# Two rows of projection unit 15 are queued ahead of the last row of unit 14

## The reference

```python
proj = x @ w_in[l]
q, fz, iv, g, u = jnp.split(proj, [D_HGRN, 2 * D_HGRN, 3 * D_HGRN, 4 * D_HGRN], axis=-1)
o_a, sa = hgrn2_mixer(q, fz, iv, g, ...)    # 4 heads of 128: gated recurrence, RMSNorm, * sigmoid(g)
o_b, sr, si = s5_mixer(u, ...)              # y = gelu(...); y * sigmoid(y @ w_glu)
mix = jnp.concatenate([o_a, o_b], axis=-1) @ w_out[l]
x = layer_norm(ALPHA * x + mix, ln1_g[l], ln1_b[l])
```

## Time and profile before

| | us |
|---|---|
| median of 3 runs | 1201.9 (1201.84 to 1202.13) |
| the profiled execution, its own time | 1201.42 |
| its span in the profile | 1199.7 |
| PE busy in the span | 1170.7 (98%) |
| DVE busy | 815.1 (68%) |
| ACT busy | 508.1 (42%) |

### The profile page before, as it was taken

The page is one execution under the profiler, slowest core; times in us unless marked ns, Lnnn a source line. Parts: engine busy times, 40 slices in busy tenths (PEclk is TensorE's granted clock), DMA queues, the critical chain, the costliest instruction groups (busy, mean ns, idle before and its releaser), DMA issues.

```text
span 1199.7 us, 24092 instructions
## 1 busy us (share of the span) xinstructions
PE 1170.7 (98%) x9718; PEld 1129.7 (94%) x9718; DVE 815.1 (68%) x1498; ACT 508.1 (42%) x850; POOL 180.2 (15%) x152
## 2 busy tenths in 40 slices
PE   9999999999898999999999999999999999999996
PEld 8988889998798999999999999999999999999995
DVE  6995767567888557799627863686458844786547
ACT  5411212337746536675314541354125521554335
POOL 5210000100000244200210021001200030001365
PEclk9999999999899999999999999999999999999999
DMA  8441223518344410411372127222631255122503
GB/s 299 118 122 50 87 79 122 175 61 225 115 109 182 178 36 26 153 37 45 86 261 90 55 64 273 97 66 55 235 137 55 56 181 190 57 57 59 207 25 119
DMA packets 84815, 139.31 MB, mean 116 GB/s; under 512 B 26360, under 2 KB 52504, under 8 KB 84696
## 3 DMA queue, kind: packets, MB, share of 16 engines
q1 hardware_dynamic: 84704, 137.77, 36.0%
HBM read 97.89 MB, written 40.03 MB: 115 GB/s over the span
## 4 chain that ended last, share of the span: by engine, by line
PE 86%; DVE 8%; ACT 2%; issue 2%; DMA 1%; POOL 0%; SPq 0%; POOLq 0%; ACTq 0%; DVEq 0%
PE psum L1984 31%; PE psum L1668 16%; PE psum L1956 15%; PE psum L1687 6%; PE psum L2067 5%; PE psum L1745 4%; PE psum L1657 1%; DVE R L2594 1%; PE psum L1798 1%; PE psum L1780 1%; PE psum L1793 1%; DMA raw<-in_w_units 1%; PE psum L1865 1%; PE psum L1827 1%; DMA raw<-in_w_up 1%
## 5 line engine op out<-in xcount | busy, mean ns | idle before, releaser
L1984 PE MATMUL psum<-XH,wh 128*128 128x258 f32 x640 | 181.4, 283 | 2.5 <-DVE TR L2599 1.5
L1984 PE MATMUL psum<-XH,wl 128*128 128x258 f32 x640 | 181.0, 283 | 0.0
L1984 PE MATMUL psum<-TR,wh 128*128 128x258 f32 x640 | 181.0, 283 | 0.0
L1984 PE MATMUL psum<-XL,wh 128*128 128x258 f32 x640 | 179.8, 282 | 0.0
L1598 POOL TENSOR_TENSOR wl<-raw,wh 128x512 fp32r<-128x512 f32 (+2 forms) x36 | 57.7, 1608 | 567.3 <-ACT wh L1273 556.6
L1984 PEld LDWEIGHTS psum<-XH,wh 128*128 128x128 f32 x640 | 121.0, 189 | 3.2 <-issue 3.2
L1956 PE MATMUL psum<-AH,wl 128*128 128x344 f32 x384 | 123.1, 320 | 0.0
L1956 PE MATMUL psum<-AL,wh 128*128 128x344 f32 x384 | 123.1, 320 | 0.0
L1956 PE MATMUL psum<-AH,wh 128*128 128x344 f32 x384 | 122.9, 320 | 0.0
L1984 PEld LDWEIGHTS psum<-XL,wh 128*128 128x128 f32 x640 | 121.5, 190 | 0.0
L1984 PEld LDWEIGHTS psum<-XH,wl 128*128 128x128 f32 x640 | 120.9, 189 | 0.0
(11 more groups left out here) (413 smaller groups left out, 2808.5 us busy)
## 6 DMA issues: line engine op xcount, KB each, us to landing
raw<-in_w_up SPq DMA_DIRECT2D x44, 512.0 KB, 4.1
ub<-rscr SPq DMA_DIRECT2D x16, 516.0 KB, 5.1
rscr<-ub SPq DMA_DIRECT2D x16, 516.0 KB, 3.4
raw<-in_w_dn SPq DMA_DIRECT2D x32, 256.0 KB, 3.4
raw<-in_w_units SPq DMA_DIRECT2D x15, 512.0 KB, 4.7
fscr<-st SPq DMA_DIRECT2D x10, 516.0 KB, 3.0
R<-in_xT SPq DMA_DIRECT2D x8, 516.0 KB, 6.4
RS<-rscr SPq DMA_DIRECT2D x8, 516.0 KB, 4.4
```

Source lines behind the costliest of these rows:

```text
L1984: ins = nc.tensor.matmul(psum[:, bank, 0:QW], a[:, k * P:(k + 1) * P], x, start=(start and p_ == 0), stop=(stop and p_ == 2), skip_group_c ...
```

## The change

Only the order in which rows of units 14 and 15 enter the queue is changed:

```diff
-    queue += unit(14, range(4)) + unit(15, range(4)) + unit(14, range(4, KD)) + unit(15, range(4, KD))
+    queue += unit(14, range(4)) + unit(15, range(4)) + unit(14, range(4, KD - 1)) + unit(15, [4, 5]) + unit(14, [KD - 1]) + unit(15, [6, 7])
```

## The result

| | before | after |
|---|---|---|
| median | 1201.87 us (4 runs, 1201.43 to 1202.13) | 1209.16 us (4 runs, 1208.21 to 1209.52) |
| ratio to before | | 1.0061, interval 1.0049 to 1.0073 |
| span of the profiled execution | 1199.7 us | 1207.8 us |
| PE busy | 1170.7 us | 1174.9 us |

A forecast was written before the change was run, and what follows sets the result against it. PE, busy 98%, was taken as the bound, with VectorE and ScalarE also on the path around the change. Delays of 4.05 + 0.85 = 4.9 us on 1201.42 gave 1206.3, plus 0.5 for the median: 1206.8 us, range 1203.3 to 1210.0.

The forecast's parts named there:

- The new order: Heads 1 to 3: two empty slots get rows 15.4 and 15.5; one row sooner over some 45 us, closing steps move forward.
- Part 1: The gaps before level 2 of head 2 and `o` of head 1, filled: low weights of unit 17 late, +0.24 us.
- Part 2: Low weights of unit 18 move ahead of the second half of `hp_a` of head 3, delaying `kt`: +0.61 us.
- Part 3: zh 1 ahead of the copy of `o` of head 2: last part of `o` late, +1.36 us.
- Part 4: Unit 18 with table loads ahead of `ms` 0 of head 2, zh 2 ahead of `ms` 2: `fin` 2 4.05 + 0.85 late.
- The sum: Whole delay through to the end: 4.05 (zh 1 and unit 18 moves included) + 0.85 = 4.9 us.
- PE's clock falls as well: Rival, 18%: waits of some 3 us twice within 357 to 375 lower the clock, +2.9 us, to 1209.7.
- The 6.4 us of the third gap: Level 5 of head 2: 3.56 us issue gap plus low clock behind it; claimed to buy nothing, VectorE being full.
- The row stays won: Rival, 16%: the bank of level 4, head 3, is not waited for; the row done sooner pays, about -0.6 to -1.7 us.
- the gap reaches the end: Rival, 6%: the level 5 gap of head 2 goes, 6.4 us come back; -1.5 us, up to -4.
- Half the delay: Rival, 14%: unit 18 ahead of `ms` 0 without zh 2 waiting for z 2; 2 to 3 us, 1204.3.

The follow-up runs named there:

- the first four runs: Changed kernel with the old list back from three ever later points, or with row 19.2 and zh 2 behind `ms` 2: 1202.12, 1202.96, 1204.26, 1206.52 us.
- back before `o`: Changed kernel with the slot before `o` of head 2 cut to one row, old list from zh 1 on: 1202.96 us for 1201.51 before.
- moved alone: Kernel before with only row 18.2 and zh 1 moved ahead of `o` of head 2: 1202.21 us for 1201.58 before.
- the ladder: Changed kernel, old list back from row 16.0, from zh 1, or from unit 18 on: +0.6, +1.5, +2.8 us; the last step adds zh 1 ahead of `o`.
- the rows in the gaps only: Changed kernel with the double slot behind the fins of head 1 cut to one, old list from row 16.0 on: 1202.12 us for 1201.51 before.
- one scale late: Kernel before with `s0_scale` of head 3 moved from between `ms` 1 and `ms` 2 to behind zh 3: 1201.15 us for 1201.69 before.

## Why the forecast held, and what it left out

- **The new order** was right in each step that the rows show, and the trace has the waits where they were put: before level 4 of head 3 (1.88 us; some 3 were said) and before row 20.2 (3.28).
- **Part 1** (+0.24 at the low weights of unit 17): they start at 327.89 for 327.36 and the profile began 0.31 us earlier, so 0.84. But that is this one execution: behind `o` of head 1 its clock was low for a while (0.52 in 309 to 312, see below), row 14.7 took longer, ScalarE waited 0.33 us for it, and the chain of ScalarE carried 0.6 us on. In the first four runs, with the same list there and the clock at 1.00, the low weights are 0.25 us late. The part was right.
- **Part 2** (+0.61): the step takes 0.62 us at 333.57, ahead of the second half of `hp_a`. The second half of `kt` starts at 337.27 for 336.14, 1.44 late counted from `kv`, of which 0.6 is again the clock of part 1; where that stayed up it is 0.84 to 0.92 late (table above). Parts 1 and 2 were put at 0.85. Right. The 1.5 us of the run back before `o` hold the low clock behind the wait as well.
- **Part 3** (+1.36 at the last part of `o`): 1.49 there when moved alone. Right in size and mechanism at that place. At `ms` 0 the forecast's own numbers leave 0.4 of it, because zh 1 is gone from there (4.95 = 1.36 + 4.58 - 0.99); measured are 0.59, and 0.6 in the median. So that the ladder's step also gives 1.3 is luck: it holds VectorE's delay by the low clock.
- **Part 4**: from the end of z 1 to the end of `ms` 2 the old list takes 366.13 - 350.35 = 15.78 us, the new one 373.16 + 0.49 - 353.33 = 20.32, 4.54 more; the forecast had 371.05 - 351.04 = 20.01, 4.2 more. Right. About 2.8 of it is unit 18 ahead of `ms` 0, some 1.1 to 1.3 zh 2 ahead of `ms` 2.
- **The sum** was 4.9 and is 7.3. The term that was mis-sized is the clock, which the sum put at nothing on the path. z 1 ends 3.29 us late for 0.70, and these 2.6 us are there before parts 3 and 4 begin: 0.6 by the low clock from 309 us on, and most of the rest by VectorE's wait for PE at 341.62, 2.16 us where 0.45 was said. The rival "PE's clock falls as well" names the right mechanism and price (+2.9) in the wrong place, and that the price fits is in part luck. It took the waits behind 357 us. There the clock did fall, to 0.57 in 377 to 381, but the low weights of unit 21, for which PE waits, end only at 379.79 + 1.23 = 381.02, so it cost 0.3 us at most. The wait that hurt is the one for `kt` at 334 to 337. The prediction had that wait, by its own figures some 0.40 + 1.43 + 0.85 = 2.7 us long, and didn't ask what the clock would do with PE's rows behind it. The forecast's range held the result because it had room for the clock at all.
- **The 6.4 us of the third gap** buy nothing that shows in the time: the rows in the gaps only. Up to 0.9 us of them were on the path, and the +0.24 of part 1 is what ScalarE's 0.95 leaves behind them. That the gap went because two more rows lie ahead of level 5 is argued from the traces alone. All kernels with the rows in the gaps are without it, and those without them have it (3.80, 3.56, 3.49, 3.21 and, with one scale late, 2.18 us).
- **The rivals.** "The row stays won" and "the gap reaches the end" are refuted by the ladder. "Half the delay" had a price of 2 to 3 us because it took unit 18 ahead of `ms` 0 for cheap; that alone costs 2.8.

## What to carry to other kernels

A gap in front of a wait isn't lost time if another engine's list is full behind it: before filling it, follow what the moved work releases. In a list that all engines share, pulling one row of matmuls forward pulls its closing steps forward too, and these can step in front of what the path waits for, with their table loads. And price a new wait twice, once for its length and once for the clock that the matmuls behind it may get.

## What was not expected of the hardware

The granted clock can fall without a wait of PE that the profile shows. In the changed kernel it was down from about 309 us, and PE had been busy for 5.86 of the 6 us before:

```profile
303.00:309.00 6.00, 5.86 (x109) 5.60 (x108) 2.90 (x4) 2.55 (x6) 0.00 (x0) 1.00 0.01 2
309.00:312.00 3.00, 3.00 (x11) 2.83 (x10) 2.93 (x4) 2.60 (x5) 0.00 (x0) 0.52 0.97 267
```

What PE did there is `o` of head 1, small matmuls of 128 columns and 16 of one column. The kernel before ran the same work with the clock at 1.00 in its profiled execution, and so did all eight other profiles of kernels with the two rows in the gaps. The kernel before with one scale late had 0.57 in 308 to 312, so it isn't a matter of the change. Where the clock falls differs from one execution to the next, one reason why differences of 1 us between such kernels can't be told from few runs.
